# Split-precision main products: two products of 256 columns into one half bank instead of one of 512 into both halves

## The reference

```python
def first_block(x, ...):                                   # x: (1, 256, 2048)
    proj = rms_norm(x, norm1_w) @ w_in                     # 2048 -> 10792
    q, kv, gates, dn_qkv, dn_z, a, b, merge_g = split(proj)
    o_nsa = nsa_mixer(rope(q), kv, gates, ...)             # compressed, selected and window attention
    o_dn = gated_deltanet(dn_qkv, dn_z, a, b, ...)         # conv, 8 heads, chunked recurrence
    g_nsa, g_dn = split(sigmoid(merge_g))
    mixed = g_nsa * (o_nsa @ w_up_nsa) + g_dn * (o_dn @ w_up_dn)
    x = x + mixed @ w_o
    h2 = rms_norm(x, norm2_w)
    return x + (silu(h2 @ w_ffn_gate) * (h2 @ w_ffn_up)) @ w_ffn_down      # 5632 wide

def second_block(x, ...):
    proj = rms_norm(x, attn_norm_g) @ w_in_2               # 2048 -> 4448
    y = concat(rwkv7_mixer(shifted parts of proj), mla_mixer(rest of proj))
    x = x + y @ w_out
    h = rms_norm(x, ffn_norm_g)
    x = x + (silu(conv3(h @ ffn_w_gate)) * (h @ ffn_w_up)) @ ffn_w_down    # 5632 wide
    return rms_norm(x, final_norm_g)
```

## Time and profile before

| | before |
|---|---|
| runs | 2802.66, 2800.72, 2800.12 us, median 2800.72 |
| profiled execution | 2797.75 us, its span 2795.9 us |
| PE busy | 2754.8 us, 99% of the span, 16660 products |
| PEld busy | 2431.0 us, 87% |
| DVE busy | 2012.8 us, 72% |
| ACT busy | 1370.3 us, 49% |
| POOL busy | 484.0 us, 17% |

### The profile page before, as it was taken

One profiled execution on the slowest core, in us unless ns is written; L12 is line 12 of the kernel. 1 busy time (PEld: TensorE's weight loads), 2 busy tenths in 40 slices (PEclk: granted clock), 3 DMA queues, 4 the chain that ended last, 5 costly groups with the idle time before them and its releaser, 6 DMA issues.

```text
span 2795.9 us, 42233 instructions
## 1 busy us (share of the span) xinstructions
PE 2754.8 (99%) x16660; PEld 2431.0 (87%) x16660; DVE 2012.8 (72%) x3057; ACT 1370.3 (49%) x2059; POOL 484.0 (17%) x526
## 2 busy tenths in 40 slices
PE   8999999999999999999999999999999999999998
PEld 7888888888888888888888888888998888888887
DVE  7987897776766666656657889868677777667655
ACT  6453555455554554444436545533554444444434
POOL 2221111100111111001102633620111111001001
PEclk9999999999999999999999999999999999999999
DMA  6544334455555555555556433321465555555555
GB/s 225 166 158 159 128 130 151 150 188 189 191 188 193 188 191 194 189 191 193 190 181 211 160 106 120 106 76 61 149 199 192 192 189 191 193 189 192 193 179 160
DMA packets 133396, 474.72 MB, mean 170 GB/s; under 512 B 14800, under 2 KB 15056, under 8 KB 132944
## 3 DMA queue, kind: packets, MB, share of 16 engines
q1 hardware_dynamic: 133200, 472.02, 51.4%
HBM read 469.87 MB, written 2.10 MB: 169 GB/s over the span
## 4 chain that ended last, share of the span: by engine, by line
PE 87%; DVE 8%; ACT 2%; POOL 1%; issue 1%; DMA 0%; SPq 0%; DVEq 0%; ACTq 0%; POOLq 0%
PE ps L957 86%; DVE ringl L1942 3%; DVE U L1942 3%; POOL U L2613 1%; DVE U L1951 1%; ACT high L1468 1%; PE ps L960 0%; DVE U L1948 0%; DVE xT L1942 0%; DVE U L2137 0%; DMA xT<-in_x_dram 0%; POOL U L2686 0%; DVE U L2225 0%; DVE hx L1942 0%; DVE U L2146 0%
## 5 line engine op out<-in xcount | busy, mean ns | idle before, releaser
L957 PE MATMUL ps<-hr,high 128*128 128x512 f32 x4672 | 1490.1, 397 | 12.1 <-DVE ringl L1942 11.0
L1942 DVE TENSOR_TENSOR ringl<-ring,high 128x1024 fp32r<-128x1024 f32 x888 | 1086.5, 1226 | 438.2 <-ACT high L1468 437.6
L1468 ACT ACTIVATE high<-ring 128x1024 fp32r<-128x1024 f32 x888 | 915.5, 1033 | 615.8 <-PE ps L957 602.8
L957 PEld LDWEIGHTS ps<-hr,ringl 128*128 128x128 f32 x4672 | 879.3, 188 | 192.4 <-issue 0.7
L957 PE MATMUL ps<-hr,ringl 128*128 128x256 f32 x4672 | 924.0, 279 | 0.0
L957 PEld LDWEIGHTS ps<-hr,high 128*128 128x128 f32 x4672 | 718.4, 188 | 21.1 <-issue 14.8
L957 PE MATMUL ps<-yur,high 128*128 128x512 f32 (+1 forms) x2432 | 681.0, 369 | 2.9 <-issue 1.6
L2613 POOL TENSOR_TENSOR U<-U,rs 128x256 f32<-128x256 f32 x292 | 272.9, 935 | 1651.7 <-DVE U L1942 1632.4
L957 PEld LDWEIGHTS ps<-yur,ringl 128*128 128x128 f32 x2176 | 399.3, 188 | 80.4 <-issue 0.7
L1468 ACT ACTIVATE U<-ps 128x256 f32<-128x256 f32 (+4 forms) x481 | 173.7, 372 | 573.1 <-PE ps L957 556.6
L957 PE MATMUL ps<-yur,ringl 128*128 128x256 f32 x2176 | 429.1, 279 | 0.0
(11 more groups left out here) (179 smaller groups left out, 1239.8 us busy)
## 6 DMA issues: line engine op xcount, KB each, us to landing
ring<-in_w_dram SPq DMA_DIRECT2D x862, 512.0 KB, 3.3
ring<-in_w_dram SPq DMA_DIRECT2D x48, 256.0 KB, 3.4
xT<-in_x_dram SPq DMA_DIRECT2D x3, 512.0 KB, 8.5
out_dram<-hx SPq DMA_DIRECT2D x3, 512.0 KB, 2.7
cst<-in_cst_dram SPq DMA_DIRECT2D x1, 1438.5 KB, 13.0
yT<-in_lora_dram SPq DMA_DIRECT2D x1, 1024.0 KB, 7.8
xT<-in_x_dram SPq DMA_DIRECT2D x2, 256.0 KB, 5.0
U<-in_lora_dram SPq DMA_DIRECT2D x1, 512.0 KB, 5.5
```

The lines of the kernel that those rows point to most:

```text
L957: return e.matmul(out, l, r, start=start, stop=stop)
L1468: return e.activation(out, i, ACT.Copy, scale=scale)
L1942: return e.tensor_tensor(out, a, b, op)
```

## The change

Every main tile takes Xh and Xl by two products of 256 columns with the same Wh into the first half of the bank, as `wout` did. The second half isn't written. `half` and `rest` go: ScalarE's copy frees the bank, GpSimd waits for that copy, VectorE adds x once for `wo` and `down`, and for `up` it multiplies the gate with PSUM itself, so that `um` and ScalarE's copy of `up` go too. The scheduler's table is adapted. The core of the diff:

```diff
-TILE, TILE4, TILE33, ROWS = 0.346, 0.432, 0.23, 0.70
+TILE, TILE4, TILE33, ROWS = 0.341, 0.432, 0.23, 0.70
...
+        def by_vector(u):
+
+            return sums_x(u) or u.kind == "up"
...
-            work["DVE"].append((m - 0.5, sum(JOIN if u.kind == "wout" else 2 * JOIN + 0.1 if sums_x(u) or u.kind == "up" else JOIN for u in then) + JOIN * later.count("up"),
-                                [("end" if sums_x(u) else "half", u.i) for u in then], [("free", u.i) for u in then]))
+            work["DVE"].append((m - 0.5, JOIN * (len(then) + later.count("up")),
+                                [("end", u.i) for u in then], [("free", u.i) for u in then]))
...
                         if n == 0 and prev is not None:
-                            c = mact if one_half(prev) else mdve
+                            c = mdve if by_vector(prev) else mact
                             e.wait_ge(c.sem, c.after("free", prev.i))
...
-                                if u.kind == "wout":
-                                    for n_, half in enumerate(moving(u, k0 + k)):
-                                        mm(out[:, 0:SEQ], wh, half, start and n_ == 0, False)
-                                else:
-                                    mm(shaped(out[:, :], 2, SEQ), wh, halves(u, k0 + k), start, False)
-
+                                for n_, half in enumerate(moving(u, k0 + k)):
+                                    mm(out[:, 0:SEQ], wh, half, start and n_ == 0, False)
...
-                copy(place_of(u), src).then_inc(mact.sem, mact.inc("free" if one_half(u) else "half", u.i))
+                copy(place_of(u), src).then_inc(mact.sem, mact.inc("free", u.i))
...
-            def rest(u, dst):
-
-                e.wait_ge(mact.sem, mact.after("half", u.i))
-                tt(dst, dst, ps[u.bank][:, SEQ:2 * SEQ], ADD).then_inc(mdve.sem, mdve.inc("free", u.i))
-
...
                     if part == 0:
-                        stt(mixT[:, t, :], s, 1.0, um[:, t % 2, :], ADD, MUL).then_inc(mdve.sem, mdve.inc("sg", t))
+                        stt(mixT[:, t, :], s, 1.0, src, ADD, MUL).then_inc(mdve.sem, mdve.inc("free", u.i))
+                        mdve.also("sg", t)
...
-                    parts = 1 if u.kind == "wout" else 2
-                    for j in range(parts):
-                        src = ps[u.bank][:, SEQ * j:SEQ * j + SEQ]
-                        if u.kind == "wo":
-                            i = stt(x, src, 0.5, x, MUL, ADD)
-                        else:
-                            i = tt(x, x, src, ADD)
...
+                if u.kind == "wo":
+                    i = stt(x, src, 0.5, x, MUL, ADD)
                 else:
-                    rest(u, place_of(u))
+                    i = tt(x, x, src, ADD)
+                i.then_inc(mdve.sem, mdve.inc("free", u.i))
...
@@ def evac0(u) of GpSimd
                 if normed(u):
-                    e.wait_ge(mdve.sem, mdve.after("free", u.i))
+                    e.wait_ge(mact.sem, mact.after("free", u.i))
```

More of the change, by code:

```diff
@@ L669, in build @@
         sg += [ar.take(SEQ), ar.take(SEQ)]
-        um = ar.take(2, SEQ)
         assert ar.at <= dn0
@@ L847, in build @@
             ends = p.ends.get(m - 1, [])
-            own = [u for u in ends if not sums_x(u)]
-            both_ = [u for u in ends if not one_half(u)]
+            own = [u for u in ends if not by_vector(u)]
+            then = [u for u in ends if by_vector(u)]
+            scaled = [u for u in ends if scaled_later(u)]
             later = [u.kind for u in p.ends.get(m - 2, [])]
@@ L975, in sums @@
                 i.then_inc(mpe.sem, mpe.inc("sum", tag))
-            def halves(u, k):
-                if u.kind in ("up", "wout"):
-                    t = 8 * u.key[0] + k if u.kind == "up" else OUT[u.key[0]][k]
-                    return both(y_high[u.kind == "wout"][t], y_at + SEQ * t)
-                if u.kind == "wo":
-                    return both(mixh_at + SEQ * k, u_at + mark1 + SEQ * k)
-                if u.kind == "down":
-                    return axr[:, 16 * (u.key[1] % 2) + k, :, :]
-                return hxr[:, k, :, :]
             def moving(u, k):
@@ L1512, in evac0 @@
                 src, key = ps[u.bank][:, 0:SEQ], u.key
-                if u.kind in ("down", "wout", "wo"):
+                if by_vector(u):
                     if summed_in(u) and (u.kind == "wout" or key[-1] == 15):
@@ L1972, in low_of_y @@
                     .then_inc(mdve.sem, mdve.inc("yl", block_, t))
-            def rest(u, dst):
-                e.wait_ge(mact.sem, mact.after("half", u.i))
-                tt(dst, dst, ps[u.bank][:, SEQ:2 * SEQ], ADD).then_inc(mdve.sem, mdve.inc("free", u.i))
             def evac0(u):
-                key = u.key
-                if one_half(u):
+                if not by_vector(u):
                     return
+                key, src = u.key, ps[u.bank][:, 0:SEQ]
+                if u.i in FIRSTS:
+                    e.wait_ge(mpe.sem, mpe.after("first", u.i))
+                else:
+                    e.wait_ge(used.sem, used.after(u.end()))
                 if u.kind == "up":
@@ L1995, in evac0 @@
                         mdve.also("sg", 16 + t)
-                elif u.kind in ("wo", "down", "wout"):
-                    x = xT[:, key[-1], :]
-                    if u.i in FIRSTS:
-                        e.wait_ge(mpe.sem, mpe.after("first", u.i))
-                    else:
-                        e.wait_ge(used.sem, used.after(u.end()))
-                    if u.kind == "wout" and key[0] == 0:
-                        e.wait_ge(ldve.sem, ldve.after("xs", key[1]))
-                    parts = 1 if u.kind == "wout" else 2
-                    for j in range(parts):
-                        src = ps[u.bank][:, SEQ * j:SEQ * j + SEQ]
-                        if u.kind == "wo":
-                            i = stt(x, src, 0.5, x, MUL, ADD)
-                        else:
-                            i = tt(x, x, src, ADD)
-                        i.then_inc(mdve.sem, mdve.inc("free", u.i) if j == parts - 1 else mdve.inc())
-                        if j < parts - 1:
-                            e.wait_ge(mdve.sem, mdve.last())
-                    if summed_in(u) not in ("", "final_g") and key[-1] == 15:
-                        low_of(summed_in(u), 15)
-                else:
-                    rest(u, place_of(u))
+                    return
+                x = xT[:, key[-1], :]
+                if u.kind == "wout" and key[0] == 0:
+                    e.wait_ge(ldve.sem, ldve.after("xs", key[1]))
+                if u.kind == "wo":
+                    i = stt(x, src, 0.5, x, MUL, ADD)
+                else:
+                    i = tt(x, x, src, ADD)
+                i.then_inc(mdve.sem, mdve.inc("free", u.i))
+                if summed_in(u) not in ("", "final_g") and key[-1] == 15:
+                    low_of(summed_in(u), 15)
             def evac1(u):
```

25 lines of the change are left out of this document (7 added, 18 removed).

## The result

The changed kernel takes 2837.9 us (median of four runs, 2835.5 to 2839.5) where the kernel before took 2801.7 beside it: a ratio of 1.0127, with a 95% interval from 1.0109 to 1.0145. It is slower by 36 us; the forecast was 41 us faster. The profiled execution took 2836.56 us, its span is 2834.8.

The account below looks back on a forecast made before the run. TensorE's product pace was taken to bound the pure stretches, with VectorE counting in the mixed ones; 24.3 + 5.6 + 7.8 + 2.9 + 0.4 = 41.0 us off the 2800.72 median gave 2759.7 us, range 2745 to 2778.

Parts of the forecast that it names:

- The pace of three products: All main tiles: three products of 256 columns cost 5.0 ns a tile less than 512 + 256; 24.3 us at full TensorE.
- The slower rival: All tiles: a fixed part for each product, or the loads, becomes the bound; about 2872 us, chance 0.04.
- The pace of `wout` is its own: Main tiles outside `wout` would not get its 0.3400 us a tile; 11.1 us remain, about 2790 us, chance 0.06.
- the second rival: Main tiles: the pace of `wout` is its own and does not carry over; about 2790 us, chance 0.06.
- The rule of the Trainium skill: All tiles: N / 2.4 + 2.5 ns a product makes three products dearer than two, an estimated 16 us of loss.
- VectorE's additions, 7.8 us: Two mixed stretches: fewer VectorE additions take 4.3 + 3.5 us off the chain; bounds nothing to 19.9 us.
- The loop, 2.9 us: Last `down` of the first block: one addition less shortens 7 whole rounds from 4.49 to 4.08 us.
- The end, 0.4 us: Last unit: one addition to x in place of two in a row (0.88 us), 0.4 us less.
- The 41 us: Whole kernel: the forecast gain, 24.3 + 5.6 + 7.8 + 2.9 + 0.4 = 41.0 us.
- the 5.6 of the mixers' stretches: Mixed stretches and start: 1644 tiles 5.0 ns faster, counted at the chain's 68% on TensorE, 5.6 us gained.

Follow-up runs that it names:

- kick_before: The kernel before with two fp32 products of 256 columns added ahead of the third unit of each feed-forward part: 2805.3 us, ratio 1.0007.
- with the kicks: The changed kernel with two added 128-column products ahead of five units of each feed-forward part and two of `wout`: 2782.9 us, ratio 0.9927.
- split_only: The kernel before with only the 512-column product split into two of 256, into the two halves; additions and waits stay: 2838.9 us, ratio 1.0137.
- short2: The changed kernel with two added 128-column products ahead of gate(1,2), gate(2,2) and wout(1,1): 2783.4 us (median of 12), ratio 0.9957.
- parts_split: The kernel before, split only in `wo` and feed-forward parts, additions kept, two 128-column products ahead of five units of each part: 2786.4 us, ratio 0.9942.
- short2_more: The changed kernel with two 128-column products at three places and thirty-six more, ahead of every second unit of seven kinds: 2799.3 us, ratio 0.9985.
- bench3: The changed kernel plus thirty quiet streams behind its end, each after four fp32 products, then two 128-column products and 36 more: some 3120 us.
- bench2: The changed kernel plus thirteen series of six quiet 36-product streams behind its end, each behind its series' added products: streams at 113.3 or 117.8 ns a product.
- short2_row: The changed kernel with two 128-column products ahead of five units of each feed-forward part and two of `wout`: 2782.9 us, ratio 0.9927.
- bench1: The changed kernel plus quiet TensorE streams behind its end, with varied operands, halves, order and widths: 256-column streams at 113.3 and 117.8 ns a product.

## Why the prediction was wrong, point by point

**The pace of three products: the step that failed.** "So three products of 256 cost 5.0 ns a tile less than 512 + 256." The forecast took 0.3400 us a tile from 64.60 us of `wout` and five triples of what it called `vs` as the pace of the form. It is one of two. Both places happened to stand at 113.3 in the profiled execution of the kernel before. A third, the first half of `vs` at 226 us of the same trace, stood at 117.8 and was not looked at; in kick_before and in the changed kernel the same `wout` stood at 117.8. At that pace a tile takes 353.3 ns, 8.3 more than the 345.0 of the earlier trace rows. The table confirms both sizes over 1800 tiles: 636.0 - 621.0 = 15.0 us is +8.3 ns a tile in the changed kernel, 621.0 - 612.0 = 9.0 us is -5.0 with the kicks. So the form can give what the forecast took for it, but only where the streams are brought to the pace that it named.

**The rivals.** The slower rival had the mechanism's threshold right: "It decides as soon as a product with its load costs over 345 / 3 = 115 ns at full rate". In most streams it costs 117.8. But the rival took this for a fixed part of each product, 12.5 ns more a tile and 2872 us in all; the very same products take 113.3 elsewhere. "The pace of `wout` is its own" was nearer in spirit and also wrong: it is not `wout`'s. Both had only 0.10 between them, because two agreeing samples of 65 and 1.7 us were taken for the form's law. The argument against the second rival, that "`vs` shows it with `hr` and three banks", rests on the products of `vw`; `vs` itself showed both paces.

**The rule of the Trainium skill** (TensorE: Matmul & The Clock Gate, section Back-to-back issue gap), N / 2.4 + 2.5 ns for a product, gives 109.2 ns at 256 columns and an estimate of 16 us of loss. The changed kernel lost, as by the rule, but not for its reason: the gaps are 113.3 or 117.8, and at 113.3 the form gains 5.0 ns a tile. In the sweep the gap from 272 columns on is N / 2.4 plus 11.7 to 15.6 ns. The same section calls the rule the gap of an isolated product and says that in a stream of loads and products both set the spacing; the flat 111.66 ns up to 240 columns fits that. Its sustained 131 ns at 512 columns is not what runs here, 228.9.

**VectorE's additions, 7.8 us: not found.** The mixers' stretches are at 560.6 us (tiles 0 to 1200) and 447.7 (4000 to 4600) with the additions gone, at 559.3 and 447.0 with them kept in split_only. In the first the chain by line is, in the changed kernel and then in split_only:

```profile
by line: PE ps L951 89.1%; PE ps L954 2.3%; DVE ringl L1917 1.7%; POOL U L2576 1.5%; DVE U L1917 1.1%; issue 0.8%; DMA ring<-in_w_dram 0.6%; ACT high L1447 0.6%; ACT hr L1447 0.4%; DVE rs L1937 0.3%; ACT U L1610 0.3%; DVE U L2326 0.3%; DVE 
```

```profile
by line: PE ps L957 82.9%; DVE ringl L1943 3.5%; DVE U L1943 2.3%; PE ps L960 1.7%; DVE U L1952 1.7%; POOL U L2614 1.5%; ACT high L1469 0.9%; issue 0.9%; DMA ring<-in_w_dram 0.6%; DVE U L1949 0.6%; ACT hr L1469 0.4%; DVE U L2370 0.4%; DVE y
```

In the kernel before TensorE had 71% and VectorE's lines 17.9% of the same window. With slower tiles TensorE takes the chain from VectorE, and then the additions count less. Both kernels have most streams at 117.8 there, so what the additions are worth at the forecast's pace is not shown. A share of a chain is not a time that can be taken off; that other work stood just short of it here is argued. In the second stretch a gain does appear, and is given back: tile 4400 comes 207.9 - 200.2 = 7.7 us earlier than in split_only, and tiles 4400 to 4600 take 8.4 us longer. The side work with which this stretch ends was no earlier, and the main tiles only got ahead and waited. Which step of the side work sets it was not taken apart.

**The loop, 2.9 us: the step held.** Tiles 3800 to 4000 take 1.7 us less in the changed kernel, although their pace alone would make them longer, and 4.3 less with the kicks, of which the pace is at most 1.0. The loop's rounds, by VectorE's timeline of short2, at four pieces a round:

```profile
1505.83 1.23 DVE L1920 TENSOR_TENSOR ringl<-ring,high 128x1024 fp32r<-128x1024 f32 x1 [1.46 <-ACT high L1450]
1506.97 0.42 DVE L1920 TENSOR_TENSOR xT<-xT,ps 128x256 f32<-128x256 f32 x1
...
1509.90 1.23 DVE L1920 TENSOR_TENSOR ringl<-ring,high 128x1024 fp32r<-128x1024 f32 x1 [1.46 <-ACT high L1450]
1511.05 0.42 DVE L1920 TENSOR_TENSOR xT<-xT,ps 128x256 f32<-128x256 f32 x1
```

4.07 us, against the 4.08 forecast. parts_split and split_only keep both additions, and with them rounds of 4.50 and 74.1 us, although TensorE needs only 4.24 us a round in both; so the addition is the cause.

**The end, 0.4 us: right.** One addition of 0.42 us stands there instead of 0.88:

```profile
2822.92 0.42 DVE L1917 TENSOR_TENSOR xT<-xT,ps 128x256 f32<-128x256 f32 x1 [3.81 <-PE ps L951]
```

**The 41 us, put together again.** With the kicks the change gives 16.1 us between the profiled executions (2797.75 and 2781.69) and 20.8 between the medians. In the table it is 14.1: 18.3 of pace in the two parts, 4.3 in the loop with its pace and 1.0 around `w_o`, less 8.8 in the mixers' first stretch, where most streams stood at 117.8 (563.2 for 554.4), and 0.6 in `wout`. The pace and the loop have the mechanism that was forecast; missing are the 7.8 that no run found, and the 5.6 of the mixers' stretches, which became a loss.

**What stays open.** What inside TensorE the two paces are, and why each third position works, no record here shows. Nor is it shown why the same kernel with one kick a part catches in nine executions and not in three. Neither was it tried to keep the first stretch at 113.3: its streams are cut by side work every few us, and the kicks of short2_more cost what they brought.

## What to carry to other kernels

A pace read in one place of a kernel is that place's pace; before it is multiplied by thousands of tiles, look for every stream of the same form in the trace, behind different neighbours (the first half of `vs` would have shown the second pace here), above all where loads and products are both full (PEld at 100%) and a margin of 1.7 ns decides. When a long stream runs a few per cent above the best that the same instructions reach, look at the gaps of starts in the trace: if they repeat a fixed rhythm, cut the stream with two short products at a few places in a row, and measure again; that took 55 us off the changed kernel for 3 us of added work. And a shorter program of an engine that holds a fifth of the chain promises nothing until the work just beside the chain is known.

## What the runs showed of the hardware

- A stream of 256-column products in fp32r, each with its own weight load of 128 x 128, has two stable paces at the full granted clock: 113.33 ns, held for up to 702 us (short2), and 117.78 ns, held for up to 746 us (after). Products of 512 + 256 columns showed one, 345.0 ns for both.
- What cuts the stream decides the pace, together with where it falls. Four fp32 products of 256 columns led to 117.8 thirty times of thirty (bench3). Two of 128 columns in such a stream led to 113.3 when the number of products ahead of them was right modulo 3, ten times of thirty (bench3). They never moved a stream off 113.3: 18 times of 18 (bench2, short2_row, short2_more, parts_split).
- The gap is 111.66 ns for 128 to 240 columns alike, and N / 2.4 plus 11.7 to 15.6 ns from 272 on (126.66 at 272, 131.66 at 288, 228.88 at 512; one stream for each width, bench1).
- A VectorE instruction of 128x256 that took 419 ns (`yur<-U,yur`) took 737 where an instruction of GpSimd had already begun (84 of 104, after); where it began first itself, it kept its 419 (84 of 104, before).
